# Entry row statistics of two x tiles moved to ScalarE, low weight parts of the first two units moved to VectorE

## The reference, cut to what matters

```python
def layer_norm(x, g, b):
    xf = x.astype(jnp.float32)
    mu = jnp.mean(xf, axis=-1, keepdims=True)
    var = jnp.mean(jnp.square(xf - mu), axis=-1, keepdims=True)
    return ((xf - mu) * lax.rsqrt(var + LN_EPS) * g + b).astype(x.dtype)
...
    hp = layer_norm(x_prompt, ln_in_g, ln_in_b)
    hs = layer_norm(x_sample, ln_in_g, ln_in_b)
    for layer in range(DEPTH):
        ...
        proj = x @ w_in + b_in
```

## Time and profile before

| what | us |
|---|---|
| median of three runs | 1096.7 |
| lowest, highest run | 1094.59, 1096.8 |
| the profiled execution's own time | 1093.59 |
| its span | 1091.8 |
| TensorE busy | 1040.2 (95%) |
| VectorE busy | 566.0 (52%) |
| GpSimd busy | 492.9 (45%) |
| ScalarE busy | 474.6 (43%) |
| start of `front` on TensorE, in the chain of waits | 32.14 |

### The profile page before, as it was taken

How to read it: one execution, slowest core, us unless ns; L and a number is a source line. 1 busy time by engine, 2 the same in 40 slices (tenths; PEclk the granted TensorE clock), 3 DMA queues, 4 the chain that set the end, 5 groups by cost and what they waited for, 6 DMA issues and landing times.

```text
span 1091.8 us, 18589 instructions
## 1 busy us (share of the span) xinstructions
PE 1040.2 (95%) x7557; PEld 921.0 (84%) x7557; DVE 566.0 (52%) x1163; ACT 474.6 (43%) x812; POOL 492.9 (45%) x334
## 2 busy tenths in 40 slices
PE   1899999998999999999999999999899999999997
PEld 1877898776889999998788599977688999999975
DVE  7438997777773111101580699877777331101137
ACT  2244335667774432223223533476777462222310
POOL 3222355453554745445434244554445474444550
PEclk9999999999999999999999999999999999999999
DMA  6621443011111223423225223321101222242322
GB/s 198 210 78 50 147 149 131 2 40 40 40 40 63 76 90 113 143 77 117 89 79 186 62 72 101 98 83 41 40 5 36 78 78 78 78 174 85 110 76 86
DMA packets 70457, 96.61 MB, mean 88 GB/s; under 512 B 4587, under 2 KB 61381, under 8 KB 69733
## 3 DMA queue, kind: packets, MB, share of 16 engines
q1 hardware_dynamic: 66068, 82.68, 23.1%
q0 software_dynamic: 3872, 11.64, 3.3%
q10 hardware_dynamic: 432, 1.11, 0.3%
HBM read 79.46 MB, written 14.78 MB: 86 GB/s over the span
## 4 chain that ended last, share of the span: by engine, by line
PE 83%; DVE 6%; ACT 3%; POOL 3%; DMA 2%; issue 2%; SPq 0%; DVEq 0%; ACTq 0%
PE ps L503 43%; PE ps L821 10%; PE ps L780 7%; PE ps L695 5%; PE ps L604 3%; PE ps L588 2%; PE ps L646 2%; PE ps L657 2%; PE ps L674 2%; DMA raw<-in_w_in 2%; POOL w_lo L1454 1%; DVE x_nat L1178 1%; PE ps L755 1%; PE ps L734 1%; PE ps L712 1%
## 5 line engine op out<-in xcount | busy, mean ns | idle before, releaser
L1454 POOL TENSOR_TENSOR w_lo<-raw,w_hi 128x1024 fp32r<-128x1024 f32 (+1 forms) x116 | 282.0, 2432 | 374.9 <-ACT w_hi L872 374.8
L503 PE MATMUL ps<-xT_hi,w_hi 128*128 128x288 f32 x960 | 284.9, 297 | 2.8 <-POOL w_lo L1454 2.8
L503 PE MATMUL ps<-xT_hi,w_lo 128*128 128x288 f32 x960 | 282.8, 295 | 0.0
L503 PE MATMUL ps<-xT_lo,w_hi 128*128 128x288 f32 x960 | 282.7, 294 | 0.0
L503 PEld LDWEIGHTS ps<-xT_hi,w_hi 128*128 128x128 f32 x960 | 180.1, 188 | 4.8 <-POOL w_lo L1454 3.4
L503 PEld LDWEIGHTS ps<-xT_lo,w_hi 128*128 128x128 f32 x960 | 180.1, 188 | 0.0
L503 PEld LDWEIGHTS ps<-xT_hi,w_lo 128*128 128x128 f32 x960 | 180.1, 188 | 0.0
L872 ACT ACTIVATE w_hi<-raw 128x1024 fp32r<-128x1024 f32 (+1 forms) x116 | 121.0, 1045 | 122.1 <-PE ps L503 72.7
L1415 DVE TENSOR_TENSOR qy<-qy,ps 128x576 f32<-128x576 f32 x32 | 24.1, 754 | 253.8 <-PE ps L503 253.8
L921 ACT ACTIVATE qy<-ps,bias 128x576 f32<-128x576 f32 x40 | 29.7, 743 | 151.6 <-PE ps L503 148.6
L1546 POOL TENSOR_TENSOR attn<-attn 128x1024 f32<-128x1024 f32 (+1 forms) x24 | 55.2, 2298 | 71.5 <-DVE attn L1350 71.5
(11 more groups left out here) (173 smaller groups left out, 2144.3 us busy)
## 6 DMA issues: line engine op xcount, KB each, us to landing
raw<-in_w_in SPq DMA_DIRECT2D x44, 1024.0 KB, 5.2
raw<-in_w_out SPq DMA_DIRECT2D x8, 1024.0 KB, 5.0
x_kept<-x_nat SPq DMA_DIRECT2D x2, 2560.0 KB, 11.6
x_nat<-x_kept SPq DMA_DIRECT2D x2, 2560.0 KB, 11.6
raw<-in_w_proj_a SPq DMA_DIRECT2D x8, 512.0 KB, 3.5
raw<-in_w_proj_b SPq DMA_DIRECT2D x8, 512.0 KB, 4.5
x_nat<-in_x_prompt SPq DMA_DIRECT2D x4, 512.0 KB, 8.5
out<-stage POOLq DMA_DIRECT2D x8, 256.0 KB, 4.9
```

Source lines behind the costliest of these rows:

```text
L503: last = mm(out, a, b[:, HALF * half:HALF * (half + 1)], start=(k == 0 and i == 0), stop=(k == n - 1 and i == 2))
L1454: g.tensor_tensor(lo, src, hi.bitcast(f32), ALU.subtract).then_inc(s_lo, 1)
```

## The change

Four things are different, all in the first layer's entry:

- VectorE takes bn_stats of x tiles 0 to 2 only. For tiles 3 and 4 ScalarE computes the moments in a new function `row_stats(t)`: a Copy over 1024 columns with an accumulated sum, the sum times -1/1024, and a Square of (x - mean) with an accumulated sum. It writes the unused outputs over `stage`. `row_stats(3)` stands after std of tile 0, `row_stats(4)` after the high parts of tile 1.
- In `layer_norm(0, 3)` and `(0, 4)` VectorE waits for `s_sq` and scales the two sums by 1/1024 in one small instruction in place of bn_aggr.
- VectorE does the low parts of units 0 and 1 in a new function `first_rest`: unit 0 between `layer_norm(0, 3)` and `x_rest(0, 2)`, unit 1 after `x_rest(0, 2)`.
- GpSimd calls `rest(0)` and `rest(1)` in layer 1 only. In layer 0 its first work is thus the seven `s_past` loads.

```diff
@@ -871,6 +876,20 @@
                 src, hi, _ = unit_views(u)
                 act_f(hi, src, ACT.Copy).then_inc(s_hi, 1)
 
+            def row_stats(t):
+
+                act.wait_ge(s_xin[t], 16)
+                n = t - 3
+                junk = stage[:, :, :].rearrange("p a n -> p (a n)")[:, 0:1024]
+                if n:
+                    act.wait_ge(s_sq, n)
+                act_f(junk, x_nat[:, t, :], ACT.Copy, accum_out=row_moments[:, n, 0:1]).then_inc(s_rowsum, 1)
+                act.wait_ge(s_rowsum, n + 1)
+                act_f(minus_mean[:, n:n + 1], row_moments[:, n, 0:1], ACT.Copy, scale=-1.0 / D).then_inc(s_minus, 1)
+                act.wait_ge(s_minus, n + 1)
+                act_f(junk, x_nat[:, t, :], ACT.Square, bias=minus_mean[:, n:n + 1],
+                      accum_out=row_moments[:, n, 1:2]).then_inc(s_sq, 1)
+
             def norm_front(L):
 
                 for t in range(6):
@@ -885,6 +904,8 @@
                             act_f(bias_all[:, :], ps[:, 0, 0:DEPTH * NBIAS], ACT.Copy).then_inc(s_biasall, 1)
                         head_of(L, 0)
                         head_of(L, 1)
+                    if t == 0 and L == 0:
+                        row_stats(3)
                     if t >= 1:
                         t0, n = TILES[t - 1]
                         for kk in range(2):
@@ -893,6 +914,8 @@
                             act_f(xT_hi[:, 4 * kk:4 * kk + 4, t0:t0 + n],
                                   ps[:, 4 + i % 4, 0:4 * n].rearrange("p (k n) -> p k n", k=4),
                                   ACT.Copy).then_inc(s_xhi, 1)
+                    if t == 2 and L == 0:
+                        row_stats(4)
 
 
             act.dma_start(ident, A["const"][:, 0, :]).then_inc(s_ident, 16)
@@ -1164,8 +1187,12 @@
             def layer_norm(L, t):
 
                 done = L * 5
-                dve.wait_ge(s_bnst, L * 10 + 5 + t + 1 if L else 2 * t + 2)
-                v.bn_aggr(mean_var[:, t, :], stats[:, t, :]).then_inc(s_mv, 1)
+                if L == 0 and t >= 3:
+                    dve.wait_ge(s_sq, t - 2)
+                    v.tensor_scalar(mean_var[:, t, :], row_moments[:, t - 3, :], 1.0 / D, None, ALU.mult).then_inc(s_mv, 1)
+                else:
+                    dve.wait_ge(s_bnst, L * 10 + 2 + t if L else 2 * t + 2)
+                    v.bn_aggr(mean_var[:, t, :], stats[:, t, :]).then_inc(s_mv, 1)
                 dve.wait_ge(s_mv, done + t + 1)
                 row = x_nat[:, t, :]
                 v.scalar_tensor_tensor(row, row, mean_var[:, t, 0:1], gb[:, 0, :], ALU.subtract,
@@ -1189,17 +1216,29 @@
                                     ps[:, 4 + i % 4, 0:4 * n].rearrange("p (k n) -> p k n", k=4), hi,
                                     ALU.subtract).then_inc(s_xlo, 1)
 
+            def first_rest(u):
+
+                dve.wait_ge(s_hi, u + 1)
+                src, hi, lo = unit_views(u)
+                v.tensor_tensor(lo, src, hi.bitcast(f32), ALU.subtract).then_inc(s_lo, 1)
+
             dve.wait_ge(s_const_b, 4)
-            for t in range(5):
+            for t in range(3):
                 dve.wait_ge(s_xin[t], 16)
                 for n in range(2):
                     v.bn_stats(stats[:, t, 6 * n:6 * n + 6], x_nat[:, t, 512 * n:512 * n + 512]).then_inc(s_bnst, 1)
             dve.wait_ge(s_gb_in, 32)
             for t in range(6):
                 if t < 5:
+                    if t >= 3:
+                        dve.wait_ge(s_xin[t], 16)
                     layer_norm(0, t)
+                if t == 3:
+                    first_rest(0)
                 if t >= 1:
                     x_rest(0, t - 1)
+                if t == 3:
+                    first_rest(1)
 
             for L in range(DEPTH):
 
@@ -1453,10 +1492,9 @@
                     src, hi, lo = unit_views(u)
                     g.tensor_tensor(lo, src, hi.bitcast(f32), ALU.subtract).then_inc(s_lo, 1)
 
-                rest(0)
-                rest(1)
-
                 if L:
+                    rest(0)
+                    rest(1)
                     pool.wait_ge(s_wo, L * 10)
                 LS = slice(L, L + 1)
                 for dst, src in ((past_i, A["cache_idx_k"]), (past_b, A["cache_dsa_k"])):
```

More of the change, by code:

```diff
@@ L188, in build @@
         one_eps = sb("one_eps", [128, 3], f32)
+        row_moments = sb("row_moments", [128, 2, 2], f32)
+        minus_mean = sb("minus_mean", [128, 2], f32)
         REGION = 19712
@@ L328, in build @@
         s_mv = sem("mean_var_ready")
+        s_rowsum = sem("row_sum_of_x_ready")
+        s_minus = sem("minus_mean_ready")
+        s_sq = sem("square_deviations_summed")
         s_std = sem("std_ready")
```

## The result

The changed kernel takes 1.0020 times as long as the kernel before (95% interval 1.0012 to 1.0028; medians 1097.79 and 1094.66 us, 16 runs each). The same kernel timed again, beside other runs of the kernel before, gave 1.0018 (1.0009 to 1.0027). By the interval that is 1.3 to 3.1 us slower, 2.2 at its middle.

What follows compares the result with a forecast made beforehand. Past the entry the kernel was taken as one long TensorE stream, bound by when front starts. Front's start +0.3 us and clock +0.4 us on 1096.7 us gave 1097.4 us, range 1093.6 to 1099.2.

Steps and rivals of the forecast that it cites:

- GpSimd's queue: Layer 0 entry: seven s_past loads, 1.38 MB, issue from about 1 us and make SyncE's loads land later.
- The size of the delay: Landing of raw1, the second weight chunk: 3.6 us later, bounds 0 and 6, from 17.4 to 21.0 us.
- How the delay comes about: SyncE's raw1 load, issued at 11.37 us, lands later because the queues take turns on the DMA engines.
- The path behind raw1: From raw1's landing through ScalarE's copies and VectorE's layer_norm, x_rest and first_rest(0) to front: 11.5 us.
- R: Moment at which raw1, the second weight chunk, lands: 17.4 us undelayed, 21.0 us with the forecast delay.
- ScalarE's slack: row_stats on ScalarE, about 2.9 us each, isn't last; row_stats(4) has 0.8 us to spare.
- TensorE's clock: At front, a gap of some 0.7 us may prolong the 1.2 GHz stretch: 0.4 us taken, bounds 0 to 0.8.
- After the start: Behind front's start, tile 4 and the third weight chunk stay covered (0.2 and 1.3 us left); no added time.
- The sum: Whole kernel: front's start +0.3 and clock +0.4 give +0.7 us, 1097.4 us.
- The band and the absolute figure: Whole kernel: likeliest -0.2 to +2.2 us, chance 0.52; 1097.4 us from a 1096.7 base, range 1093.6 to 1099.2.

Runs made afterwards that it cites:

- kernel 1: Changed kernel with GpSimd's seven layer-0 loads held until the second weight chunk (raw1) has landed; ratio 0.9974 to the kernel before.
- kernel 2: Kernel before, with only GpSimd's seven layer-0 loads moved ahead of its two low parts; ratio 1.0034 to the kernel before.
- Kernel 6: Changed kernel with GpSimd's first four loads (64 KB each) early, the others held until raw1 has landed; ratio 0.9989 to the kernel before.
- kernel 9: Changed kernel with SyncE's load of raw1 issued ahead of the eight loads of bias rows; ratio 1.0028 to the kernel before.
- kernel 10: kernel 5 with SyncE's load of raw1 ahead of the bias rows too; ratio 0.9986 to the kernel before.
- kernel 8: The changed kernel timed again without any edit; ratio 1.0018 to the kernel before.
- kernel 4: Changed kernel with first_rest(0) moved into VectorE's idle time ahead of x_rest(0,0); ratio 1.0001 to the kernel before.
- kernel 3: Changed kernel with the low parts of units 0 and 1 given back to GpSimd, ahead of its loads; ratio 0.9968 to the kernel before.
- kernel 5: Changed kernel with GpSimd's loads held until raw1 has landed, first_rest(0) before x_rest(0,0), first_rest(1) after layer_norm(0,4); ratio 0.9963, median 1090.56 against 1094.50 us.

## Why the prediction was right, point by point

**GpSimd's queue: right, and it decided.** The seven loads went at 1.3 to 6.5 us and ate the whole gain, as put. Kernels 1 and 2 show it from both sides: one wait takes 4.6 us off the start of `front`, and the loads alone put 4.6 on.

**The size of the delay: 3.6 put, 4.4 measured** (`raw1` at 21.8 in place of 17.4), within the bounds 0 to 6. Nearest was the time that the packets took when alone (4.1), then the 3.9 of layer 1, and the bytes at full rate (3.3) were furthest off. The 3.6 that I took lay between the last two. Kernel 6 speaks for the packet time too: 1.1 us by it, 1.4 measured (the second w_hi at 18.65 against 17.23 in kernel 1).

**How the delay comes about: partly wrong.** I had `raw1` issued at 11.37 in any case and landing late. It landed 6.1 us after its issue, as before; it was the issue that came 4.3 us late, since SyncE stood in a load of bias rows. The sum holds all the same, since the landing did not hang on when SyncE came to the load: issued 11.4 us earlier, in kernel 9, `raw1` lands at 21.7 again, and in kernel 10 at 17.2 as in kernel 1. What goes through the engines ahead of it is the same. But the step matters for repairs: what stands behind the standing instruction comes late, `raw1` in one order and the bias rows in the other. The Trainium skill's rule of turns ("DMA: Bandwidth & Descriptors", "Queues, rings and completion order") is now seen with GpSimd's queue too: 52.7% and 50.7% in 12 to 14 us.

**The path behind raw1: right.** R + 11.5 put; 33.01 - 21.78 = 11.2 measured, and 11.2 in kernels 1 and 8 too. `first_rest(0)` took 0.76 us (0.8 put), the gap ahead of `front` was 0.65 us (0.7 put).

**ScalarE's slack: right.** `row_stats(4)` took 2.6 us (2.9 put) and ended at 27.87, R + 6.1 (R + 6.7 put). What it could hold up is std of tile 3, which stands behind it on ScalarE; its own sums VectorE wants only for tile 4, at 33.91. Std of tile 3 starts at 28.19, after ScalarE has been idle for 0.31 us, released by VectorE's small scaling instruction at 27.99. VectorE takes the reciprocal of it at 29.39, so with the 0.29 us of std some 1.2 us were to spare, where I had put 0.8.

**TensorE's clock: term of 0.4 us with bounds 0 to 0.8; measured 0.4 and 1.45 in two profiles of the same kernel.** The reason that I gave, the gap, is not borne out: kernel 4 has no gap and 5.32 us, kernel 8 has the gap and 4.74. Over the twelve profiles the 24 matmuls took 4.7 to 6.0 us in the six with the gap and 4.2 to 5.3 in the six without. The ranges overlap, and one kernel differs from itself by 1.1 us, so a part of 0.4 us can neither be shown nor ruled out. The working had 4.2 us for the kernel before, where the earlier trace rows have 4.37.

**After the start: right up to unit 3.** The 2.3 us between the two kernels at `front`'s second stretch (39.70 against 37.38) are 2.4 at unit 3 (58.71 against 56.30), so neither tile 4 nor the third chunk cost more.

**The sum.** +0.7 put, +2.2 measured. The start of `front` is +0.9 to +1.0 where I had +0.3 (the 0.8 us that the delay was put too low, less 0.2 of the path), and the first 24 matmuls are +0.4 in kernel 8's profile, as put. Together that is 1.3 to 1.4 us, and both groups of times have moved by 1.2 to 1.4 (last section). The other 0.8 us of the ratio is in how often the upper group came; I had no term for that. The span of kernel 8's profile is 2.3 us longer than that of the kernel before: 1.5 of it is there at unit 3 (57.76 against 56.30), 0.4 is a weight load at layer 1's entry that took longer (17.29 against 16.89), and some 0.4 is not taken apart.

**The band and the absolute figure: in part luck.** A delay of 3.3 to 5.2 us with 0 to 0.8 of clock gives 0.0 to +2.7 us by my own terms, not the -0.2 to +2.2 that I wrote. The measured 2.2 lies inside the one and on the edge of the other, and the interval lies wholly above 1, where my likeliest answer was a change that can't be told from none. That 1097.4 came so near the measured 1097.79 is luck: I had started from 1096.7, the median of three runs of which two were in the upper group, and sixteen runs give 1094.66.

## What to carry to other kernels

Before work is taken off an engine, look at what that work was holding back on the engine's queue. Two subtractions on GpSimd were an unwritten gate that kept 1.4 MB of DMA out of the busiest 17 us of the kernel; with the gate written out as a wait, the same change is worth 2.8 us in place of a loss of 2.2. With the two subtractions left where they were and only the statistics moved, which needs no new wait, it is 3.5 us (kernel 3), and with the wait and one subtraction in idle time 4.0 us (kernel 5). The intervals of these three overlap, so which is the best is not shown; kernel 3 is the smallest change. And where a load bounds the path, a subtraction moved into the wait for it took nothing from the path, while behind it it counted in full (kernel 4: 0.74 of 0.76 us).

## What the runs showed of the hardware

**A DMA instruction on SyncE stood for 4.6 to 9.7 us.** Eight loads of bias rows took 7.0 to 7.4 us of SyncE with its own and ScalarE's queue in the engines, 8.6 with 0.26 MB more on GpSimd's queue, and 11.0 to 11.5 with 1.38 MB more. It is one instruction of the eight that stands (4.64 us in the kernel before, 8.77 in the chain above), SyncE's seventh DMA; in kernel 9 the seventh is the load of `raw1`, and that one stands for 9.74 us. Whether the number of DMAs under way or their bytes make it stand, no run shows.

**TensorE's lower level beyond the entry.** In both profiles below TensorE had just done the eight L471 matmuls of `rel_rows` (2.77 us, from 123.91 in the first and 122.97 in the second) and gone on with full units. Windows of 4 us (us, busy of each engine, granted clock, DMA), first the changed kernel:

```profile
122.00:126.00 4.00, 4.00 (x22) 3.02 (x21) 3.83 (x9) 2.05 (x4) 0.29 (x1) 1.00 0.00 0
126.00:130.00 4.00, 4.00 (x19) 3.46 (x18) 3.86 (x7) 1.21 (x4) 2.07 (x1) 0.65 0.17 28
```

then the same kernel again (8):

```profile
122.00:126.00 4.00, 4.00 (x18) 2.47 (x17) 3.83 (x8) 3.00 (x6) 1.23 (x1) 1.00 0.00 0
126.00:130.00 4.00, 4.00 (x33) 4.00 (x32) 3.86 (x8) 0.27 (x1) 1.15 (x1) 1.00 0.40 101
```

In the first the granted clock falls to a mean of 0.65 in 126 to 130 us (half, the 1.2 GHz level, from 127.2 to 130.6 by the trace's record), where TensorE does 19 matmuls against 33 in the second. The next block of 48 matmuls after it starts at 141.68, 3.9 us later than in the kernel before (137.76), where unit 3 was 2.4 later. The two programs are the same; the clock had risen in `front` at 38.5 us in the first and at 36.2 in the second. By the trace's record of the granted clock, counted from that rise, this dip begins 88.7 us on in the two profiles that show it (the changed kernel's and kernel 4's; kernel 9's has one at 78.5), and later ones begin 228.7 us on in eleven of the twelve profiles and 754.3 us on in all twelve. That the moment of the rise brings in or leaves out the dip 90 us later would fit this, but it is not shown: no run sets that moment on purpose.

**What it does to times.** The runs of most of these kernels fall in two groups some 2.4 us apart, and the upper has the lower mean granted clock: of kernel 8's eleven, seven took 1095.2 to 1096.1 us at 0.995 to 0.996 and four 1097.7 to 1098.3 at 0.992 to 0.994. The kernel before has the same two groups, near 1094.5 and 1096.8. So of the 2.2 us that the change costs, 1.2 to 1.4 is the shift of both groups, in either measurement; the other part is how often the upper group comes: 11 of 16 runs against 4 of 16 in the first, 4 of 11 against 5 of 27 in the second. That the change makes it come more often is not shown, for beside kernels 1 to 4 the kernel before had it itself in 11 of 24. That the dips make the groups is likely from the clocks, but not shown: only one run of each is profiled.
